# Filter spectra formed for even and odd tokens apart, the last modulation group in two parts, and another order in the first stage

## What is computed

```python
cond = silu(c)
mod = cond @ w_ada + b_ada                 # 6 parts of 2048
sh1, sc1, g1, sh2, sc2, g2 = split(mod, 6)
h = x * (1.0 + sc1) + sh1
z_u, z_v, z_h, z_g = split(h @ w_in + b_in, ...)
filt = hyena_filters(...)                  # from positions and small weights alone
...
k_spec = two_sided_spectrum(filt[:, 0, n], filt[:, 1, n])
y = gate * (irfft(rfft(y, n=512) * k_spec)[:256] + y * skip)
```

## Time and profile before

| | |
|---|---|
| median of 3 runs | 2633.13 us (2633.02 to 2635.64) |
| the profiled execution | 2630.96 us |
| its span, first to last instruction | 2629.6 us |
| PE busy | 2597.2 us, 99% |
| DVE busy | 1845.6 us, 70% |
| ACT busy | 1289.7 us, 49% |
| HBM, over the span | 227 GB/s |

### The profile page before, as it was taken

How to read it: one execution, slowest core, us unless ns; L and a number is a source line. 1 busy time by engine, 2 the same in 40 slices (tenths; PEclk the granted TensorE clock), 3 DMA queues, 4 the chain that set the end, 5 groups by cost and what they waited for, 6 DMA issues and landing times.

```text
span 2629.6 us, 31620 instructions
## 1 busy us (share of the span) xinstructions
PE 2597.2 (99%) x12546; PEld 2169.0 (82%) x12546; DVE 1845.6 (70%) x1927; ACT 1289.7 (49%) x1566; POOL 32.1 (1%) x55
## 2 busy tenths in 40 slices
PE   7999999999999999999999999999999999999999
PEld 3789988878888888888888888888888888988887
DVE  9978989988876644687776767756554665666565
ACT  2455444444444444555555544444444654545463
POOL 0000000000000000000000000000000000000000
PEclk9999999999999999999999999999999999999999
DMA  9998877798688755666555665555655556634554
GB/s 399 382 371 303 305 283 286 273 338 315 238 297 283 247 185 188 193 204 203 192 192 193 192 191 177 192 190 184 211 192 192 183 185 172 177 125 160 192 177 143
DMA packets 276584, 598.65 MB, mean 228 GB/s; under 512 B 21264, under 2 KB 46288, under 8 KB 260064
## 3 DMA queue, kind: packets, MB, share of 16 engines
q1 hardware_dynamic: 268272, 566.52, 63.2%
q0 software_dynamic: 4560, 21.56, 2.5%
q10 hardware_dynamic: 3616, 8.68, 0.8%
HBM read 586.24 MB, written 10.49 MB: 227 GB/s over the span
## 4 chain that ended last, share of the span: by engine, by line
PE 89%; DVE 7%; DMA 2%; issue 1%; ACT 1%; ACTq 0%; DVEq 0%; SPq 0%
PE ps L951 26%; PE ps L953 26%; PE ps L952 26%; DVE group_acc L2390 2%; PE ps L1076 2%; DVE w_lo L2271 2%; PE ps L1060 2%; PE ps L1063 1%; PE ps L1062 1%; DMA raw<-in_k_in 1%; PE ps L1461 1%; PE ps L1463 1%; PE ps L1462 1%; DMA raw<-in_w_in 1%; DVE ada_acc L2299 1%
## 5 line engine op out<-in xcount | busy, mean ns | idle before, releaser
L2271 DVE TENSOR_TENSOR w_lo<-raw,w_hi 128x1024 fp32r<-128x1024 f32 x870 | 1050.3, 1221 | 663.0 <-ACT w_hi L1607 661.0
L1607 ACT CAST w_hi<-raw 128x1024 fp32r<-128x1024 f32 x870 | 906.8, 1051 | 1074.5 <-PE ps L953 900.2
L951 PE MATMUL ps<-w_lo,x_hi 128*128 128x512 f32 x2592 | 1019.5, 393 | 6.6 <-DVE w_lo L2271 2.8
L953 PE MATMUL ps<-w_hi,x_lo 128*128 128x512 f32 x2592 | 1010.7, 390 | 0.0
L952 PE MATMUL ps<-w_hi,x_hi 128*128 128x512 f32 x2592 | 1010.0, 390 | 0.0
L951 PEld LDWEIGHTS ps<-w_lo,x_hi 128*128 128x128 f32 x2592 | 487.4, 188 | 111.9 <-DVE w_lo L2271 4.6
L953 PEld LDWEIGHTS ps<-w_hi,x_lo 128*128 128x128 f32 x2592 | 487.1, 188 | 102.1
L952 PEld LDWEIGHTS ps<-w_hi,x_hi 128*128 128x128 f32 x2592 | 487.6, 188 | 99.8 <-issue 1.0
L2299 DVE SCALAR_TENSOR_TENSOR ada_acc<-raw,cond,ada_acc 128x2048 f32<-128x2048 f32 x64 | 150.1, 2345 | 2.5 <-DMA raw<-in_w_ada 1.5
L951 PE MATMUL ps<-w_lo,pooled_hi 128*128 128x512 f32 x384 | 150.3, 391 | 0.0
L953 PE MATMUL ps<-w_hi,pooled_lo 128*128 128x512 f32 x384 | 149.5, 389 | 0.0
(11 more groups left out here) (379 smaller groups left out, 2135.9 us busy)
## 6 DMA issues: line engine op xcount, KB each, us to landing
raw<-in_w_m SPq DMA_DIRECT2D x128, 1024.0 KB, 5.2
raw<-in_w_ada SPq DMA_DIRECT2D x64, 1024.0 KB, 6.0
raw<-in_pool_w_in SPq DMA_DIRECT2D x64, 1024.0 KB, 5.3
raw<-in_w_in SPq DMA_DIRECT2D x56, 1024.0 KB, 7.3
raw<-in_k_mod SPq DMA_DIRECT2D x32, 1024.0 KB, 7.3
raw<-in_pool_w_out SPq DMA_DIRECT2D x32, 1024.0 KB, 5.0
raw<-in_ple_w_gate SPq DMA_DIRECT2D x32, 1024.0 KB, 5.1
raw<-in_mla_w_in SPq DMA_DIRECT2D x24, 1024.0 KB, 5.1
```

The costliest lines, as they stand in the source:

```text
L951: mm(bank, xh, wl, start=start, stop=False)
L953: ins = mm(bank, xl, wh, start=False, stop=stop)
L1607: nc.scalar.copy(by_ktile(st, w_hi[st.half_slot(j, half)][:, 0:n]), raw_half(st, j, half)).then_inc(hi_split, 1)
L2271: tt(by_ktile(st, w_lo[slot][:, 0:n]), raw_half(st, j, half), by_ktile(st, w_hi[slot][:, 0:n].bitcast(F32)), ALU.subtract).then_inc(lo_spl ...
```

## The change

1. The spectra are no longer summed over even and odd tokens on PE. `spectrum` makes 2 products of 128 x 512 instead of 4, one for the even and one for the odd tokens, each over 128 frequencies. Where `spec` is used, DVE forms the sum of both (`filter_low`) and their difference (`filter_high`) ahead of halves 9 and 10 of each round of `in_g`; both wait for their own end before the next instruction. The DFT tables shrink: the load in the first stage from 512 to 256 KB, the one on POOL's queue the same.
2. The last modulation group comes in two parts, called 3 and 4, of 256 columns: 4 pieces each, each piece holding four K tiles, so that DVE makes four multiplications of 128 x 512 of it. `group_sum` makes 4 products for these instead of 8. The weights of group 3 are laid out anew: the units (3, 0) and (3, 1) hold the K tiles 12 and 13 of all four chunks, (3, 2) and the unit of `in_vu` the K tiles 14 and 15.
3. The order of the first stage is another on SP, PE, ACT and DVE. On PE ten halves of weights stand ahead of `group_sum(2)`, where it was nine. The second addition for `ada_acc` in `in_vu` no longer stands behind the last `vu_out`, and the statistics (`sgu_norm`) and `split_dft(0)` move from ahead of half 8 of `in_h` to ahead of 9 and 11.

```diff
-    w_mod = a["w_ada"][0][:, 0:2 * D].reshape(KT // 2, 2, P, 2, 4, CH)
+    w_mod = a["w_ada"][0][:, 0:2 * D].reshape(KT // 2, 2, P, 2, 4, CH).transpose(4, 0, 2, 1, 3, 5)
+    w_mod = w_mod.reshape(4, KT // 2, P, UNIT)
+    w_mod[3] = a["w_ada"][0][:, 0:2 * D].reshape(KT // 4, 4, P, 2, 4, 2, S)[:, :, :, :, 3].transpose(4, 0, 2, 1, 3, 5) \
+        .reshape(KT // 2, P, UNIT)
     w_in = np.stack([a["w_in"][0][:, col:col + CH] for col in IN_COLS[0:4]])
+    w_in = w_in.reshape(4, 4, 4, P, CH).transpose(0, 1, 3, 2, 4).reshape(4, 4, P, UNIT)
+    w_in[:, 3] = w_in[:, 3].reshape(2, 2, P, 2, 2 * CH).transpose(3, 0, 2, 1, 4).reshape(4, P, UNIT)
     return {
-        "k_mod": w_mod.transpose(4, 0, 2, 1, 3, 5).reshape(4, KT // 2, P, UNIT),
-        "k_in": w_in.reshape(4, 4, 4, P, CH).transpose(0, 1, 3, 2, 4).reshape(4, 4, P, UNIT),
+        "k_mod": w_mod,
...
-FIRST_W = [(0, 0), (0, 1), (0, 2), (1, 1), (1, 0), (1, 2), (0, 3), (2, 1),
-           (2, 0), (1, 3), (2, 2), (2, 3), (3, 0), (3, 2), (3, 1)]
+FIRST_W = [(0, 0), (0, 1), (1, 1), (1, 0), (0, 2), (1, 2), (1, 3), (0, 3),
+           (2, 3), (2, 2), (2, 1), (2, 0), (3, 0), (3, 1), (3, 2)]
+CHUNK_FIRST, PART_LAST = [(0, 0), (0, 1), (0, 2), (1, 3)], (2, 3)
...
     def group_ada(q, u):
-        return nth_load("g", 8 * q + u)
+        return nth_load("g", 8 * q + u - 4 * (q > 3))
 
     def first_half(q, c, half):
         return ST["first"].half(0, group_weights(q, c)) + half + 1
+
+    def last_unit(n):
+        return (ST["first"], group_weights(3, n)) if n < 3 else (ST["in_vu"], 0)
+
+    def last_done(c):
+        stage, j = last_unit(2 + c // 2)
+        return stage.half(0, j) + c % 2 + 1
+
+    def added(pieces):
+        return 2 * min(pieces, 24) + 4 * max(pieces - 24, 0)
...
@@ -1113,29 +1137,34 @@
 
         def spectrum(it, m):
             pe.wait_ge(filt_win, 2 * it + m + 1)
-            for f in range(2):
-                for t in range(2):
-                    ins = mm(ps[:, spec_bank(it, m) + f, :], dft[:, m, t, f * P:(f + 1) * P],
-                             (h_sum, h_dif)[m][:, t, :], start=t == 0, stop=t == 1)
+            for t in range(2):
+                ins = mm(ps[:, spec_bank(it, m) + (1 - t if m else t), :], dft_f[:, m, t, :], (h_sum, h_dif)[m][:, t, :],
+                         start=True, stop=True)
             ins.then_inc(spec_mm, 1)
 
         def group_sum(q):
-            pe.wait_ge(group_added, 8 * (q + 1))
-            for n in range(8):
+            pe.wait_ge(group_added, 16 * (q + 1))
+            for n in range(8 if q < 3 else 4):
                 ins = mm(ps[:, sum_bank(q), n:n + 1], group_acc[q % 2][:, n * P:(n + 1) * P], ones[:, 0:1],
                          start=True, stop=True)
             ins.then_inc(group_summed, 1)
 
         st = ST["first"]
 
-        def group_half(q, c, half, first=None, last=None):
+        def group_half(q, c, half):
             pe.wait_ge(fm_lo if half else h_lo, q + 1)
             products(st, 0, group_weights(q, c), half, 4 * q + 2 * half, x_hi, x_lo, pair(c),
-                     q == 0 and half == 0 if first is None else first, q == 3 and half == 1 if last is None else last)
-
-        def group_unit(q, c, first=None, last=None):
-            group_half(q, c, 0, first, False if last is not None else None)
-            group_half(q, c, 1, False if first is not None else None, last)
+                     half == 0 and (q, c) in CHUNK_FIRST, half == 1 and (q, c) == PART_LAST)
+
+        def group_unit(q, c):
+            group_half(q, c, 0)
+            group_half(q, c, 1)
+
+        def last_half(n, half):
+            c, part = 2 * (n % 2) + half, n // 2
+            pe.wait_ge(fm_lo if part else h_lo, 4)
+            stage, j = last_unit(n)
+            products(stage, 0, j, half, 12 + 2 * part, x_hi, x_lo, pair(c), c == 3 and part == 0, part == 1)
...
         pe.wait_ge(part_kept, 1)
         group_sum(3)
+        group_unit(2, 1)
+        group_unit(2, 0)
+        last_half(0, 0)
+        last_half(0, 1)
         pe.wait_ge(mod_group, 4)
-        group_unit(2, 3, True, False)
-        group_unit(3, 0)
-        group_unit(3, 2)
-        group_unit(3, 1)
-        st = ST["in_vu"]
-        for n, j in enumerate(j for j, kind in enumerate(st.pattern) if kind == "w"):
-            for half in range(2):
-                products(st, 0, j, half, 4 * 3 + 2 * half, x_hi, x_lo, pair(3), False, half == 1)
+        group_sum(4)
+        last_half(1, 0)
+        pe.wait_ge(mod_group, 5)
+        last_half(1, 1)
+        last_half(2, 0)
+        last_half(2, 1)
+        last_half(3, 0)
+        last_half(3, 1)
...
-        def add_first(q, u):
+        def add_part(q, u, e):
 
             st, j = ST["first"], group_ada(q, u)
-            dve.wait_ge(raw_full[st.slot(j)], st.landed(0, j))
-            if u:
-                dve.wait_ge(group_added, 8 * q + u)
+            if e == 0:
+                dve.wait_ge(raw_full[st.slot(j)], st.landed(0, j))
+            parts = 2 if q < 3 else 4
+            k, n = parts * u + e, 4 * CH // parts
+            if k:
+                dve.wait_ge(group_added, 16 * q + k)
             elif q >= 2:
                 dve.wait_ge(group_summed, q - 1)
-            buf = group_acc[q % 2]
-            for e in range(2):
-                part = raw[st.slot(j)][:, e * 2 * CH:(e + 1) * 2 * CH]
-                gain = cond[:, 2 * u + e:2 * u + e + 1]
-                if u + e == 0:
-                    ins = tsc(buf[:], part, gain, None, ALU.mult)
-                else:
-                    ins = stt(out=buf[:], in0=part, scalar=gain, in1=buf[:], op0=ALU.mult, op1=ALU.add)
-                if e == 0:
-                    then(ins)
+            buf = group_acc[q % 2][:, 0:n]
+            part = raw[st.slot(j)][:, e * n:(e + 1) * n]
+            gain = cond[:, k:k + 1]
+            if k == 0:
+                ins = tsc(buf, part, gain, None, ALU.mult)
+            else:
+                ins = stt(out=buf, in0=part, scalar=gain, in1=buf, op0=ALU.mult, op1=ALU.add)
             ins.then_inc(group_added, 1)
 
...
+            n = 4 if q < 3 else 2
+            part = slice(4 * q, 4 * q + 4) if q < 3 else slice(2 * q + 6, 2 * q + 8)
...
+        add_part(4, 3, 2)
+        add_part(4, 3, 3)
+        group_rest(3, 1)
+        group_rest_half(3, 2, 0)
+        group_scale(4)
+        group_rest_half(3, 2, 1)
...
-        def in_h_2():
-            vu_out(3)
-            add_ada(ST["in_vu"], 0, 2, 2, 1)
-
-        def in_h_8():
-            sgu_norm()
-            split_dft(0)
-
-        run_at(ST["in_h"], 0, {2: in_h_2, 8: in_h_8, 12: lambda: conv_sides(0)},
+        run_at(ST["in_h"], 0, {1: lambda: vu_out(2), 2: lambda: add_ada(ST["in_vu"], 0, 2, 2, 1), 4: lambda: vu_out(3), 9: lambda: sgu_norm(), 11: lambda: split_dft(0), 12: lambda: conv_sides(0)},
...
+        def filter_low(n):
+
+            dve.wait_ge(spec_in, 16 * (n + 1))
+            then(tt(spec[:, 0:4:2], spec[:, 0:4:2], spec[:, 1:4:2], ALU.add))
+
+        def filter_high(n):
+
+            then(stt(out=spec[:, 1:4:2], in0=spec[:, 1:4:2], scalar=-2.0, in1=spec[:, 0:4:2], op0=ALU.mult, op1=ALU.add))
...
-            run_at(st, i, {4: lambda: in_g(i, 0), 8: lambda: signal_rest(i), 12: lambda: in_g(i, 1),
+            run_at(st, i, {4: lambda: in_g(i, 0), 8: lambda: signal_rest(i), 9: lambda: filter_low(i),
+                           10: lambda: filter_high(i), 12: lambda: in_g(i, 1),
```

355 lines of the change are left out of this document (191 added, 164 removed).

## The result

| | before | with the change |
|---|---|---|
| median of 8 runs each | 2634.74 us (2633.02 to 2636.91) | 2639.80 us (2638.98 to 2642.72) |
| ratio of the runs | | 1.0027, 95% interval 1.0017 to 1.0036 |
| profiled execution | 2630.96 us | 2640.77 us |
| its span | 2629.6 us | 2639.5 us |

The kernel is slower, by 0.27% or some 7 us by the ratio (interval 4.5 to 9.5 us; the two medians lie 5.1 us apart), where 0.19% faster was forecast.

The account below looks back on a forecast made before the run. DVE was taken to bound the kernel to about 95 us, then PE. First stage and `in_h` -8.4 and `in_g` +3.3 made -5.1: 2625.9 us from the profiled 2630.96, 2628.0 with 2.2 to the median; range 2623.5 to 2636.0.

Parts of the forecast that it names:

- What bounds the kernel: DVE bounds up to the end of the third modulation group, about 95 us; from then on PE, with small waits.
- the sign set beforehand: `in_h` starts near 158.8 us instead of 165.69; if it stays over 163, E.
- E: Rival: first stage gives little, as loads are the real limit or the clock falls; 2632 us, chance 0.20.
- From 95 us to `in_h`: Fewer stalls and smaller last sums on PE bring `in_h` to 158.4 us, 7.3 us less; 6.9 gained after the tie.
- The tie at DVE's end: DVE's last multiplication ends at 137.5 to 141.2 us, PE wants it at 141.2; 0.4 us taken off.
- `in_vu` and `in_h`: Earlier `ada_acc` addition and later statistics remove three PE waits, 2.0 us, less 0.5 for halves late next.
- The spectra on PE: In 0 to 95 us, some 14 us of PE work saved where PE waits for DVE anyhow; worth nothing by itself.
- `in_g`: DVE gets some 2.56 us more in each of four rounds, idle time covers part; PE loses 3.3 us, bounds 0 and 10.2.
- D: Rival: DVE becomes the bound of `in_g`, 12.6 us lost there, first stage 6 gained; 2639.7 us, chance 0.12.
- The sum: First stage and `in_h` -8.4 us, `in_g` +3.3, together -5.1; 2628.0 us at the median.
- E's second way: The clock drops behind one of the last group's two new sums, costing 1.6 us each time.

Follow-up runs that it names:

- a_vu2: Changed kernel with `vu_out(2)` on DVE ahead of half 0 of `in_h` instead of half 1; ratio to before 1.0022.
- a_short_early: Changed kernel with shortened weight loads, the two spectra stores moved to about 104 and 118 us, and `vu_out(2)` ahead of half 0 of `in_h`; ratio to before 1.0013.
- b_end: Kernel before with only the moves around `in_h`: second `ada_acc` addition ahead of the last `vu_out`, `sgu_norm` and `split_dft(0)` later; ratio to before 1.0000.
- b_part1: Kernel before with only the spectra formed apart and combined on DVE in `in_g`, old order, last group whole; ratio to before 1.0030.
- a_undo1: Changed kernel with the spectra summed on PE again and nothing added on DVE in `in_g`; ratio to before 1.0021.
- a_f12: Changed kernel with `filter_low` and `filter_high` both behind `in_g(i, 1)`, ahead of half 12 instead of halves 9 and 10; ratio to before 1.0035.
- b_cut: Kernel before with the 16 multiplications of 128 x 1024 of group 3 each made as two of 128 x 512; ratio to before 1.0011.
- a_no_filter: Changed kernel without `filter_low` and `filter_high`, so the result is not the reference's; ratio to before 1.0008.
- a_short: Changed kernel with weight units (2, c) and (3, 0) to (3, 2) loading only their first 1024 columns (result not the reference's); ratio to before 1.0022.
- b_short: Kernel before with weight units of groups 2 and 3 loading only their first 1024 columns (result not the reference's); ratio to before 0.9987.

## Why the prediction was wrong

- **What bounds the kernel.** "From then on PE sets the time, with small waits" is the step that failed. It was so in the kernel before: PE was busy 68.04 of 70 us from 95 to 165 us and came to `in_h` without a wait. But the next limit lay close behind. The DMA engines were at 0.97 of the time, and `in_h`'s first half could be ready at 162.7 us, 3 us ahead of PE. The new order has `in_h` start 3.5 us behind the landing of that load, and PE waits there: it landed at 163.7, 161.4 and 160.6 us in the three kernels that are the same up to there, and PE waited 3.7, 2.4 and 2.5 us. a_vu2 and a_short_early show that the wait is for the load. By the sign set beforehand (`in_h` over 163 us) it is E. I had noted 0.98 for the DMA share in the first row I read, and put it into rival E with a chance of 0.20.
- **From 95 us to `in_h`, forecast -6.9.** Measured +1.5 in the pair of profiles, and between -1.6 and +1.5 with the scatter. By its own terms: `group_sum(2)` 0.6 late; 3.8 us of stalls up to the sum of the last part (145.7 - 95.8 = 49.9 for 46.1 of work: a sum of 1.7, one of 0.85, 16 halves) where I had left 0.4; 4.3 us up to the start of `in_h`, 3.7 of them for `vu_out(2)` and the load behind it, where I had none. That `vu_out` behind a `w_lo` is also an added wait that I did not follow up, though the order showed it.
- **The tie at DVE's end.** I put its last multiplication at 137.5 to 141.2 us; it ended at 144.8. Cutting took 3.8 and not 1.6 us (the narrow multiplication is 0.75 us long, not 0.69), and data came late (four waits on loads of `k_mod` from 95 to 145 us, 2.7 us). The forecast's 137.5 with 2.2 more for the cutting and the old order's 3.7 of waits would have been 143.4.
- **`in_vu` and `in_h`, forecast -1.5.** Measured +1.2. b_end shows why the part of it that was right in mechanism gave nothing: the slot came free earlier, the load did not land earlier. In the changed kernel SP still issued nothing from 160.9 to 171.7 us, where I had said that this gap would go, and PE waited once more, 1.6 us. The clock at its half level from 168.2 us on costs 1.5 us there (4.30 us for a half in place of 2.76), more than the +1.2.
- **The spectra on PE, forecast 0.** Right: b_part1. But a_undo1 shows that it is 0 in the old order alone; the new one would have been 6 us late at 95 us without it.
- **`in_g`, forecast +3.3.** Measured +7.5 in the pair and 6.1 between the means. PE's waits for `w_lo` from 350 to 560 us rose from 2.7 to 9.2 us, between the 6 of the forecast and the 12 of D. The sign and the cause (DVE some 2.5 us more a round) were right, the cover was too large: the third round paid all of it, and the idle time there was a wait for data that moved along with the work and did not pay. It stopped between the forecast and rival D's 10.2, which a_f12 came close to.
- **The sum.** First stages -8.4 forecast and +2.7 measured; `in_g` +3.3 and +7.5; in all -5.1 and +9.8 (by the means of the stages +8.2, in timed runs +7). What happened is in kind E and D together. I had priced D with a first stage that gains 6 us, and E with an `in_g` that costs 3.3; that both go wrong was outside my range. Even E's first stage, with its wait of 4 us, still gained 4.4. D's price, 2639.7 us, is the measured median by luck: its `in_g` was to lose 12.6 and its first stages to gain 6. E's second way, the clock falling behind one of the new sums, did not happen: it was at 1.00 from 95 to 165 us.

The stretch of 2067 us behind `in_g` is the same in all kernels, as was said.

Open: how much the changed kernel really loses ahead of `in_g` (some 2 us, hardly more than the scatter), and what part of it is its order and what the cutting. b_cut shows 2.9 us for the cutting in the old order, within wide bounds; a kernel with the new order and an uncut group was not made. Open too is why bytes saved and stores moved give so little apart: each kernel has one profiled execution, and where the clock falls differs from one to the next. None of the kernels that leave nothing out beat the kernel before, and the experiments point to none that would.

## What to carry to other kernels

Where one engine is busy 97% of a stretch, look whether the loads are too: compare the landing of the next stage's first load with the time at which you forecast that stage to start, before any stall is counted as gain. Idle time did not pay for added work where it was a wait for data that the same engine's progress fetches; work put directly before a chain that everyone waits for costs nearly its full price. Take the price of an instruction from rows of the very form, its operands included. And look where the clock falls in each of two profiles before a difference of 1 or 2 us between them is given to an edit.

## What was not expected of the hardware

DVE slows down while POOL computes: a `w_lo` half of 1.22 us took up to 3.41 us beside POOL's instructions on tiles of 128 x 1024, and 1.33 on the mean in `in_g`. Moving 2.56 us of DVE work a round to an idle engine gave back nothing.

After 3.7 us of waiting at the start of `in_h`, PE's granted clock was 0.76 over the next 7 us, and the first half there took 4.30 us from first to last product, against 2.76 in the next ones. The waits of 1.0 and 1.4 us at 115 and 134 us had no such effect. But the length of the wait doesn't decide it alone. At the start of `in_h` the clock fell after waits of 3.69 (changed), 2.42 (a_no_filter) and 2.33 us (a_undo1), and not after 3.10 (a_short), 2.53 (a_f12) and 2.03 (a_vu2). In the old order it fell behind the last group's sum, with a wait of 0.26 us behind that sum, whether the wait ahead of the sum was 1.46 us (before), 0.40 (b_end) or none (b_part1), and not in b_short (0.17). The Trainium skill ("TensorE: Matmul & The Clock Gate", section "Why this matters for your kernels") says that gaps between bursts cost clock; the trace agrees at the start of `in_h`, and these kernels show that it comes and goes between like gaps.
